# Gathering x1 with its root's inverse and weighting expert rows inside the blocks, in a mixture-of-experts decoder step

## The chip, the cores and the metric

One core of a Trainium2 chip runs the whole step as one program. The metric is device time in microseconds, the median of the runs of one kernel; lower is better.

## What is computed

The kernel is one decoder layer on 576 tokens (512 prompt tokens and 8 x 8 sample tokens) of width 1024, all in fp32:

```
h = rmsnorm(x) * g_mix;  proj = h @ w_in                      # 1024 -> 2560
z_a = b_a * conv3(c_a * v_a);  z_b = silu(layernorm(conv31(v_b * sigmoid(g_b)) + bias))
x1 = x + concat(z_a, z_b) @ w_out
t = rmsnorm(x1) * g_ffn
group = argmax(t @ w_coarse);  two best of that group's 8 experts by t @ w_fine
p = softmax(two best) * softmax(coarse)[group]
x2 = x1 + sum over the two experts e of p_e * ((silu(t @ w_gate[e]) * (t @ w_up[e])) @ w_down[e])
y = rmsnorm(x2) * g_final
```

There are 32 experts of inner width 256: gate, up and down are 1 MB each, 96 MB in all. Four conv histories are outputs as well.

## The kernel before, in words

The semaphores and the order of each engine's instructions are written out by hand; there is no scheduler. The program has these stages.

1. Projection, convolutions and LayerNorm, to about 186 us.
2. Output projection (TensorE), x1 = x + product (DVE), and for each of the five row tiles t of x1: squares and root (ACT), transposes and router logits (TensorE), the choice of experts (DVE), to about 254 us. ACT writes x1 to memory (`x1_rows`, L688), scales it into the normed row h2 with its columns permuted (L712), and writes that too (`h2_rows`, L716).
3. Routing: token-expert rows are sorted into blocks of 64 slots, 30 blocks in this run (of at most 49, `NBLK`). `gidx` says which half row of h2 each of the 128 partitions of a block gathers (64 tokens x 2 halves), `sidx` to which half row of `y_rows` it is scattered. Each token has two y rows, k = 0 and k = 1. The fillers of `keep_busy` (L1457) occupy TensorE between its tasks.
4. The blocks. POOL gathers half rows into `stage[b]` (L887, an indirect DMA; b is the block's number modulo 2). DVE moves a stage to `xrow` (`move`, L1383), TensorE transposes it (`tokens`, L1698), DVE scales it by g_ffn into `xT` (L1387). TensorE multiplies by gate and up (L1707 for a block of one expert, L1712 for one with two), ACT takes SiLU (L748), DVE multiplies (L1394), TensorE transposes (L1722), DVE copies (L1396), TensorE multiplies by down (L1732), ACT copies the result to `yblk[b]` (L752) and POOL scatters it (L917). The expert weights come through eight slots (`places`); SP loads a slot again once its last block is through (`reload`), 24 of 32 experts in this way. The slot in `z` (number 4) shares its rows with `xT`, so its gate and up are loaded in pieces of 1 KB.
5. The end: SP loads x1 back (`xf`, L571), the final gain (L572), the y rows k = 0 once all but the last pair's blocks are scattered (unless a token has both experts in the last pair) and k = 1 once all are (L581). DVE adds for tiles 0 and 4 (`add_row`, L1424); TensorE adds for tiles 1, 2 and 3 by products with the identity (L1786) and with diagonals of the weights (L1794). ACT squares (L775), DVE norms in the order 0, 1, 4, 2, 3 (`normed`, L1437), SP stores (L587).

What sets the order around the change: on SP, loads stand in one queue in program order. On POOL, in a round of the blocks the gather for block g + 4 stands ahead of the scatter of block g. On DVE a round is `block_of`, `tokens_out`, `move`. Lines of the code to which the steps refer:

```
def load_part(i, part, e):                    # L467 (down), L469 (gate, up)
def move(q, b):                               # L1379 to L1383
dve.wait_ge(s_gath[b], q * 16 + 16)
nc.vector.tensor_copy(xrow, stage[b]).then_inc(s_mv, 1)
pool.wait_ge(s_mv, h * 2 + (b + 3))           # POOL's round
gather(h * 2 + (b + 4), b)
scatter(h * 2 + b, b, h * 2 + (b + 2))
```

## Time and profile before

| | |
|---|---|
| median of 3 runs | 518.27 us (517.01 to 520.26) |
| the profiled execution | time 519.05 us, span 517.3 us |
| TensorE busy | 473.6 us, 92% of the span |
| VectorE (DVE) busy | 265.0 us, 51% |
| ScalarE (ACT) busy | 99.9 us, 19% |
| GpSimd (POOL) busy | 193.4 us, 37% |
| read and written | 137.19 MB and 15.53 MB |
| mean granted TensorE clock | 0.985 |

Busy time is that of single engines and overlaps. The span is the part of the execution that the profile covers; the time has a small launch part beside it. A window row gives for each engine its busy time and, in brackets, its instructions. The share of DMA is the mean busy share of the core's 16 DMA engines, and can come out a little over 1.

### The profile page before, as it was taken

To read this page: it belongs to the slowest core of one execution; us is meant where nothing else is said; L and a number is where in the kernel's file an instruction comes from. 1 tells how busy PE (TensorE), PEld (TensorE's weight loads), DVE (VectorE), ACT (ScalarE), POOL (GpSimd) and SP (SyncE) were. 2 spreads that over 40 slices of the span, in tenths; PEclk is the share of its full clock that TensorE was granted. 3 is DMA by queue.
4 is the path that set the end of the run, shared out by engine and by line. 5 is a ranking of instruction groups with operands and counts; after the bars stand their busy time and mean duration, and the time that the engine had idled before them with its cause. 6 is when DMAs were issued, how large, how long until landed. Compare 5 with 4: busy or idle time off the path is not lost.

```text
span 517.3 us, 8897 instructions
## 1 busy us (share of the span) xinstructions
PE 473.6 (92%) x3253; PEld 280.8 (54%) x3254; DVE 265.0 (51%) x559; ACT 99.9 (19%) x202; POOL 193.4 (37%) x289
## 2 busy tenths in 40 slices
PE   7999999999999999999689989999979998989874
PEld 4887777777777735544434434444434444435321
DVE  4209999999999955656841222112212221221226
ACT  5140010110112424324601110111101101110204
POOL 3010925685679830003244433443333334433100
PEclk9989999999999999999699999999999999999999
DMA  8796004300000199869969999999999999999996
GB/s 327 232 378 147 1 3 176 149 1 0 1 0 1 50 384 421 303 223 342 422 272 424 415 415 387 394 407 420 415 386 418 421 420 419 399 405 424 339 322 227
DMA packets 43810, 146.01 MB, mean 282 GB/s; under 512 B 10226, under 2 KB 18434, under 8 KB 32507
## 3 DMA queue, kind: packets, MB, share of 16 engines
q1 hardware_dynamic: 37258, 131.42, 66.1%
q0 software_dynamic: 4960, 9.45, 4.9%
q10 hardware_dynamic: 1561, 4.70, 2.4%
q8 instruction: 22, 0.36, 0.3%
q14 instruction: 9, 0.07, 0.0%
HBM read 137.19 MB, written 15.53 MB: 295 GB/s over the span
## 4 chain that ended last, share of the span: by engine, by line
PE 70%; DMA 10%; issue 7%; DVE 5%; POOL 4%; SPq 2%; ACT 2%; DVEq 0%; POOLq 0%; ACTq 0%
PE banks L1501 26%; PE banks L1712 10%; PE banks L1732 9%; PE banks L1707 9%; PE banks L1559 8%; DMA region_w<-in_w_in 3%; DMA region_x<-in_w_up 2%; DMA region_w<-y_rows 2%; PE banks L1722 2%; PE banks L1588 2%; DVE region_m L1394 2%; DVE region_m L1396 1%; ACT region_m L748 1%; PE banks L1664 1%; DVE slot L1437 1%
## 5 line engine op out<-in xcount | busy, mean ns | idle before, releaser
L1501 PE MATMUL banks<-region_m,region_w 128*128 128x256 f32 (+1 forms) x576 | 141.7, 409 | 0.0
L1501 PEld LDWEIGHTS banks<-region_m,region_w 128*128 128x128 f32 x576 | 110.3, 192 | 30.6 <-issue 0.4
L1394 DVE TENSOR_TENSOR region_m<-region_m,banks 128x128 f32<-128x128 f32 x30 | 8.6, 288 | 159.8 <-ACT region_m L748 159.8
L1030 DVE SCALAR_TENSOR_TENSOR z<-region_m,z 128x512 f32<-128x512 f32 x60 | 49.1, 819 | 0.0
L1030 DVE SCALAR_TENSOR_TENSOR region_x<-region_m,region_x 128x512 f32<-128x512 f32 x56 | 45.8, 818 | 0.0
L825 POOL TENSOR_TENSOR region_m<-region_x 128x512 f32<-128x512 f32 x4 | 20.6, 5138 | 62.0 <-ACT region_m L639 31.8
L1732 PE MATMUL banks<-region_w,region_m 128*32 128x512 f32 x272 | 40.3, 598 | 2.8 <-DVE region_m L1396 2.8
L898 POOL COPY gcol<-gidx 128x1 uint32 (+1 forms) x30 | 5.4, 179 | 95.2 <-DVE region_m L1383 95.2
L627 ACT ACTIVATE region_x<-banks 128x256 f32<-128x256 f32 (+1 forms) x40 | 14.2, 406 | 120.7 <-PE banks L1501 103.6
L887 POOL DMA_INDIRECT region_x<-h_rows,gcol x30 | 31.6, 1052 | 15.2 <-issue 15.2
L752 ACT ACTIVATE region_m<-banks 128x512 f32<-128x512 f32 x30 | 17.9, 597 | 93.6 <-PE banks L1732 93.6
L1707 PE MATMUL banks<-region_w,z 128*64 128x256 f32 x288 | 34.6, 391 | 0.0
L917 POOL DMA_INDIRECT y_rows<-region_m,scol x28 | 28.9, 1032 | 15.1 <-issue 15.1
L1712 PE MATMUL banks<-region_w,z 128*32 128x256 f32 x384 | 30.7, 389 | 0.0
L398 POOL TENSOR_SCALAR region_m<-region_m 128x128 f16<-128x128 f32 x7 | 6.8, 976 | 62.9 <-DVE region_m L1173 49.6
L1559 PE MATMUL banks<-region_w,z 128*128 128x512 f32 x64 | 28.7, 597 | 0.9 <-POOL z L866 0.9
L1707 PEld LDWEIGHTS banks<-region_w,z 128*64 128x64 f32 x288 | 19.6, 134 | 18.3 <-issue 7.5
L748 ACT ACTIVATE region_m<-banks 128x128 f32<-128x128 f32 x30 | 8.3, 277 | 109.7 <-PE banks L1712 66.1
L1732 PE MATMUL banks<-region_m 128*32 128x512 f32 x176 | 25.0, 598 | 1.5 <-DVE region_m L1396 1.5
L1698 PE MATMUL banks<-ident,region_m 128*128 128x128 f32 x124 | 25.2, 286 | 0.5 <-DVE region_m L1383 0.5
L1387 DVE TENSOR_TENSOR z<-banks,gexp 128x512 f32<-128x512 f32 x31 | 21.4, 692 | 0.8 <-PE banks L1698 0.8
L843 POOL TENSOR_TENSOR region_m<-region_x 128x512 f32<-128x512 f32 x4 | 11.7, 2916 | 22.7 <-ACT region_x L627 22.7
(267 smaller groups left out, 704.3 us busy)
## 6 DMA issues: line engine op xcount, KB each, us to landing
region_w<-in_w_down SPq DMA_DIRECT2D x16, 1024.0 KB
region_w<-in_w_gate SPq DMA_DIRECT2D x12, 1024.0 KB, 9.7
region_w<-in_w_up SPq DMA_DIRECT2D x12, 1024.0 KB
region_m<-in_w_down SPq DMA_DIRECT2D x12, 1024.0 KB
region_w<-in_w_in SPq DMA_DIRECT2D x4, 2048.0 KB, 15.8
region_m<-in_w_gate SPq DMA_DIRECT2D x8, 1024.0 KB
region_m<-in_w_up SPq DMA_DIRECT2D x8, 1024.0 KB
region_w<-in_w_out SPq DMA_DIRECT2D x1, 4096.0 KB, 12.9
```

The lines of the kernel that those rows point to most:

```text
L825: pool.tensor_tensor(ub[:, c, HB:HB + SEQ], sv[:, 0:SEQ], sg[:, 0:SEQ], ALU.mult)
L887: pool.indirect_dma_start(stage[b], None, h2_half, bass.IndirectOffsetOnAxis(ap=rows, axis=0), bounds_check=2 * NTOK - 1, oob_is_err=False ...
L917: pool.indirect_dma_start(y_half, bass.IndirectOffsetOnAxis(ap=rows, axis=0), yblk[b], None, bounds_check=4 * NTOK - 1, oob_is_err=False). ...
L1030: last[j % 2] = conv(nc.vector.scalar_tensor_tensor(out=acc[j % 2], in0=ub[:, c, j:j + SEQ], scalar=wB(c, j), in1=acc[j % 2], op0=ALU.mult ...
L1387: nc.vector.tensor_tensor(xT.rearrange("p (h k) n -> p k h n", h=2), ps[0][:, :].rearrange("p (k h n) -> p k h n", k=KC // 2, h=2), gexp[: ...
L1394: nc.vector.tensor_tensor(hid, sg_m, ps[1][:, P:2 * P], ALU.mult).then_inc(s_hid, 1)
L1501: ins = mm(ps[2 * bank + j][:, 0:LEN[j]], sec[name][:, k, c * P:(c + 1) * P], hT[:, k, CUT[j]], start=(k == 0), stop=(k == KC - 1))
L1559: ins = mm(ps[bank][:, :], rows[:, k, :], cols[:, k, :], start=(start and k == 0), stop=(stop and k == KH - 1))
L1698: ins = tr(ps[0][:, k * P:(k + 1) * P], xrow[:, k * P:(k + 1) * P], ident[:, :])
L1707: ins = mm(ps[1][h * T:(h + 1) * T, 0:2 * P].rearrange("p (w f) -> p w f", w=2), xT[:, k, :], wgu[halves[0]][:, :, k, h, :], start=(k == 0 ...
L1712: ins = mm(ps[1][r0:r0 + H, 0:2 * P].rearrange("p (w f) -> p w f", w=2), xT[:, k, half * H:(half + 1) * H], wgu[i][:, :, k, h, :], start=( ...
L1732: ins = mm(ps[3][quarter * H:(quarter + 1) * H, :], hidT[:, c * T + r0:c * T + r0 + H], wdn[halves[quarter % 2]][:, c, h * 512:(h + 1) * 512],
```

## The change

h2 and its rows in memory go. x1 gets rows of 516 words per half: 512 of x1 and four that hold the inverse of its root (the row's normalizing factor). A block gathers such half rows. DVE's `move` takes its columns with a stride of four and multiplies by the factor; ACT copies x1 out of the stage into a PSUM bank (`hold`) so that the stage comes free. ACT's copy of the down product scales each row by its token's weight (`w_row`, found before the blocks by ten matmuls of the lists), DVE adds the held x1 (`add_x1`), and POOL scatters after that. So y rows are x1 + 2 p y, and the end adds two of them: 2 x2, whose final norm has four times the epsilon. The reload of x1, the diagonals and the identity products of x1 are gone.

Since a half of x1 now has features 0 to 511 or 512 to 1023, where a half of h2 had a permuted set, the rows of gate and up are assigned to partitions in two halves, `(h p k)` for `(p k)`: a partition of a load is two pieces of 4 KB where it was one of 8 KB. The slot in `z` still has pieces of 1 KB, now in two DMAs per part.

```diff
-            parts = (a["w_gate"][0].rearrange("e (p k) f -> p e (k f)", k=KC),
-                     a["w_up"][0].rearrange("e (p k) f -> p e (k f)", k=KC),
+            parts = (a["w_gate"][0].rearrange("e (h p k) f -> p e h (k f)", h=2, k=KC // 2),
+                     a["w_up"][0].rearrange("e (h p k) f -> p e h (k f)", h=2, k=KC // 2),
...
-            for t in FINISH:
-                sp.dma_start(xf[0:TROWS[t], t, :], x1_dram[t * P:t * P + TROWS[t], :]).then_inc(s_xf[t], 16)
...
-                nc.scalar.activation(h2[0:n, t % 2, :].rearrange("r (k p) -> r k p", k=KC),
-                                     x1[0:n, t, :].rearrange("r (p k) -> r k p", k=KC), ACT.Copy,
-                                     scale=small[0:n, 32 + t:33 + t]).then_inc(s_h2, 1)
-                act.wait_ge(s_h2, t + 1)
-                act.dma_start(h2_dram[t * P:t * P + n, :], h2[0:n, t % 2, :]).then_inc(s_h2d[t % 2], 16)
+                act.dma_start(x1_dram[t * P:t * P + n, :, :], x1[0:n, t, :, :]).then_inc(s_x1d[t], 16)
...
+            def hold(q, b):
+                act.wait_ge(s_gath[b], q * 16 + 16)
+                if not isinstance(q, int) or q:
+                    act.wait_ge(s_ya, q * 2 + b)
+                nc.scalar.activation(held[b], stage[b][:, 0:HD], ACT.Copy).then_inc(s_held, 1)
...
-                nc.scalar.activation(yblk[b], ps[3][:, :], ACT.Copy).then_inc(s_yc, 1)
+                nc.scalar.activation(yblk[b], ps[3][:, :], ACT.Copy,
+                                     scale=w_row[:, q * 2 + b:q * 2 + b + 1] if isinstance(q, int) else w_row[:, bass.ds(q * 2 + b, 1)])                  .then_inc(s_yc, 1)
...
                 for b in range(2):
-
+                    scatter(h * 2 + b, b, h * 2 + (b + 2))
                     pool.wait_ge(s_mv, h * 2 + (b + 3))
+                    pool.wait_ge(s_held, h * 2 + (b + 3))
                     gather(h * 2 + (b + 4), b)
-                    scatter(h * 2 + b, b, h * 2 + (b + 2))
...
-                nc.vector.tensor_copy(xrow, stage[b]).then_inc(s_mv, 1)
+                nc.vector.tensor_scalar(xrow.rearrange("r (k p) -> r k p", k=KC // 2),
+                                        stage[b][:, 0:HD].rearrange("r (p k) -> r k p", k=KC // 2),
+                                        stage[b][:, HD:HD + 1], None, ALU.mult).then_inc(s_mv, 1)
+
+            def add_x1(q, b):
+                dve.wait_ge(s_held, q * 2 + (b + 1))
+                dve.wait_ge(s_yc, q * 2 + (b + 2))
+                nc.vector.tensor_tensor(yblk[b], yblk[b], held[b], ALU.add).then_inc(s_ya, 1)
...
-            keep_busy(14)
+            pe.wait_ge(s_ohw, 1)
+            pe.wait_ge(s_wq, 1)
+            for i in range(2 * NT):
+                n = TROWS[i // 2]
+                ins = mm(ps[3][:, 0:NBLK], ohw[0:n, i, :], wq[0:n, i, :], start=(i == 0), stop=(i == 2 * NT - 1))
+            ins.then_inc(s_wsum, 1)
+            keep_busy(8)
...
-                nc.vector.scalar_tensor_tensor(out=xf[0:n, t, :], in0=yg[k][t][0:n, :],
-                                               scalar=w12[0:n, k * NT + t:k * NT + t + 1],
-                                               in1=xf[0:n, t, :], op0=ALU.mult, op1=ALU.add)\
-                    .then_inc(s_fin if k else s_fin1, 1)
+                nc.vector.tensor_tensor(xf[0:n, t, :], yg[0][t][0:n, :], yg[1][t][0:n, :], ALU.add).then_inc(s_fin, 1)
```

SP also waits for `w_row` before it loads the last slot (number 7), whose place the lists of the weights occupy.

What stands on DVE in one of the two turns of the loop over blocks, before (L1394 and L1396 are the hidden product and the copy of its transpose, L1387 the tokens' scaling, L1383 the move; names are places in memory, `banks` is PSUM):

```order
L1394 TENSOR_TENSOR region_m<-region_m,banks 128x128
L1396 COPY region_m<-banks 128x128
L1386 REGISTER_ALU
L1387 TENSOR_TENSOR z<-banks,gexp 128x4x2x64
L1380 ISA
L1382 REGISTER_ALU
L1383 COPY region_m<-region_x 128x512
```

The same turn on DVE after the change (L1426, L1428, L1419 and L1408 in the same parts, L1415 is `add_x1`):

```order
L1426 TENSOR_TENSOR region_m<-region_m,banks 128x128
L1428 COPY region_m<-banks 128x128
L1418 REGISTER_ALU
L1419 TENSOR_TENSOR z<-banks,gexp 128x4x2x64
L1415 TENSOR_TENSOR region_m<-region_m,banks 128x512
L1405 ISA
L1407 REGISTER_ALU
L1408 TENSOR_SCALAR region_m<-region_x 128x512
```

The move now stands behind an addition that needs the block's down product and ACT's copy of it.

On POOL, one turn of the loop over blocks before (L898 to L887 are the gather, L906 to L917 the scatter):

```order
L898 COPY gcol<-gidx 128x1
L900 TENSOR_TENSOR carry<-carry 128x1
L887 DMA region_x<-h_rows,gcol 128x512
L905 REGISTER_ALU
L906 ISA
L906 COPY scol<-sidx 128x1
L908 TENSOR_TENSOR carry<-carry 128x1
L917 DMA y_rows<-region_m,scol 2304x512
```

And after it (L928 to L939 are the scatter, L920 to L909 the gather):

```order
L928 COPY scol<-sidx 128x1
L930 TENSOR_TENSOR carry<-carry 128x1
L939 DMA y_rows<-region_m,scol 2304x512
L956 REGISTER_ALU
L920 ISA
L920 COPY gcol<-gidx 128x1
L922 TENSOR_TENSOR carry<-carry 128x1
L909 DMA region_x<-x_rows,gcol 128x516
```

The scatter now stands ahead of the gather.

## Rows read from the trace of the kernel before

**Rows 1.** Windows, the stretch of the blocks: engines' busy time, clock, DMA share, GB/s.
```profile
263.00:487.00 224.00, 201.67 (x2138) 97.08 (x2136) 48.47 (x129) 25.63 (x59) 83.82 (x179) 1.00 1.01 405
```

**Rows 2.** The page, packets of all DMAs.
```profile
DMA packets 43810, 146.01 MB, mean 282 GB/s; under 512 B 10226, under 2 KB 18434, under 8 KB 32507
```

**Rows 3.** Windows of 4 us: PE, PEld, DVE, ACT, POOL, clock, DMA share, GB/s.
```profile
262.00:266.00 4.00, 2.64 (x23) 1.30 (x25) 1.45 (x3) 0.00 (x0) 2.73 (x8) 1.00 0.50 148
...
278.00:282.00 4.00, 4.00 (x36) 1.74 (x33) 0.76 (x2) 0.60 (x1) 1.83 (x6) 1.00 1.02 424
...
310.00:314.00 4.00, 3.78 (x33) 2.08 (x29) 0.29 (x1) 0.47 (x2) 2.11 (x4) 1.00 1.04 354
314.00:318.00 4.00, 3.83 (x47) 1.76 (x51) 1.24 (x3) 0.60 (x1) 1.61 (x4) 1.00 1.09 381
...
334.00:338.00 4.00, 3.46 (x28) 1.06 (x24) 1.53 (x4) 0.36 (x2) 0.41 (x3) 1.00 0.85 311
...
478.00:482.00 4.00, 3.87 (x56) 1.74 (x60) 1.02 (x3) 0.60 (x1) 0.58 (x2) 1.00 1.01 417
482.00:486.00 4.00, 3.48 (x47) 1.58 (x42) 1.52 (x5) 0.28 (x1) 0.61 (x1) 1.00 1.04 317
```

**Rows 4.** Windows, same columns, while only w_out is loaded.
```profile
88.00:92.00 4.00, 4.00 (x18) 3.16 (x17) 3.90 (x6) 0.71 (x2) 3.94 (x4) 1.00 1.02 407
```

**Rows 5.** The chain that ended last: start, us, what.
```profile
453.11 12.41 DMA region_x<-in_w_up
...
488.49 4.86 DMA y_rows<-region_m,slast
...
494.29 11.49 DMA region_w<-y_rows
```

**Rows 6.** Timeline of one block: start, us, engine, line, operation, idle before.
```profile
472.87 3.84 PE L1707 MATMUL banks<-region_x,z 128*64 128x256 f32 x32
473.01 0.60 ACT L752 ACTIVATE region_m<-banks 128x512 f32<-128x512 f32 x1 [3.08 <-PE banks L1732]
473.05 1.05 POOL L887 DMA_INDIRECT region_x<-h_rows,gcol  x1 [0.50 <-issue]
475.11 1.03 POOL L917 DMA_INDIRECT y_rows<-region_m,scol  x1 [0.54 <-issue]
...
476.75 0.44 PE L1698 MATMUL banks<-ident,region_m 128*128 128x128 f32 x2
```

**Rows 7.** Groups by line and shape: count, busy us, mean ns, idle before.
```profile
L1387 DVE TENSOR_TENSOR z<-banks,gexp 128x512 f32<-128x512 f32 x31 | 21.4, 692 | 0.8 <-PE banks L1698 0.8
L1383 DVE COPY region_m<-region_x 128x512 f32<-128x512 f32 x32 | 13.4, 418 | 3.3 <-DMA region_x<-h_rows,gcol 1.9 <-DMA region_x<-h_rows,gidx 1.5
...
L712 ACT ACTIVATE region_m<-region_m,small 128x1024 f32<-128x1024 f32 x4 | 8.6, 2158 | 0.0
L695 ACT ACTIVATE region_m<-region_m 128x1024 f32<-128x1024 f32 x4 | 4.2, 1057 | 34.1 <-DVE region_m L1101 34.1
```

**Rows 8.** Timeline: the third gather and the move that waited for it.
```profile
264.95 1.05 POOL L887 DMA_INDIRECT region_x<-h_rows,gcol  x1 [0.52 <-issue]
...
273.18 0.43 DVE L1383 COPY region_m<-region_x 128x512 f32<-128x512 f32 x1 [1.87 <-DMA region_x<-h_rows,gcol]
```

**Rows 9.** Timeline of the end.
```profile
481.61 1.01 POOL L917 DMA_INDIRECT y_rows<-region_m,slast  x1 [0.54 <-issue]
...
489.50 6.44 SPq L581 DMA_DIRECT2D region_w<-y_rows  x10
...
505.81 1.27 DVE L1424 SCALAR_TENSOR_TENSOR slot<-region_w,w,slot 64x1024 f32<-64x1024 f32 x1 [2.16 <-DMA region_w<-y_rows]
...
512.75 1.28 DVE L1437 SCALAR_TENSOR_TENSOR slot<-banks,small,slot 128x1024 f32<-128x1024 f32 x1
```

**Rows 10.** Timeline of TensorE ahead of the first block.
```profile
260.21 3.19 PE L1457 MATMUL banks<-ident,onesb 128*128 128x512 bf16 x14
...
263.89 0.66 PE L1698 MATMUL banks<-ident,region_m 128*128 128x128 f32 x4 [0.48 <-DVE region_m L1383]
```

More of the change, by code:

```diff
@@ L38 @@
 QR = NS * HB // 2
+HD, XS = D // 2, D // 2 + 4
 NP = KB + KA + 3
@@ L534, in _ @@
             load_part(6, 1, 6)
-            for i in range(2):
-                sp.wait_ge(s_h2d[i], 16 * ((NT + 1 - i) // 2))
             sp.wait_ge(s_x1d[NT - 1], 16)
@@ L1402, in _ @@
             move(0, 1)
-            with nc.vector.Fori(0, pairs) as q:
+            for b in range(2):
+                block_of(0, b)
+                tokens_out(b + 2)
+                add_x1(0, b)
+                move(1, b)
+            with nc.vector.Fori(1, pairs) as q:
                 for b in range(2):
```

189 lines of the change are left out of this document (101 added, 88 removed).

## The prediction

> **What bounds the kernel now.** I read the windows first, then the DMA rates on a fine grid, then the chain of waits and the timeline of one block, and last the end of the span.
>
> From 263 to 487 us, where the 30 blocks run, the DMA engines are busy for the whole time (share 1.01, 405 GB/s) while TensorE is busy for 201.7 of 224 us [rows 1]. Both are near full, but it is the transfers that lead: in the chain, a block waits from 453.11 for an expert's up matrix that lands 12.41 us after its issue [rows 5]. The fine grid shows what the stream does: 424 and 417 GB/s where gate, up and down matrices come in plain form [rows 3]. Each is 1 MB, 8 KB per partition, and 11,303 of the 43,810 packets have 8 KB or more [rows 2]; the code has 96 x 128 - 8 x 128 = 11,264 such rows, so one row is one packet. The two windows in which the slot in `z` is loaded, whose rows are pieces of 1 KB, have 354 and 381 [rows 3]. Once (334 to 338) the stream runs dry for want of a free slot: share 0.85, 311 GB/s, that is (420 - 311) x 4 / 420 = 1.0 us lost.
>
> Behind the blocks DMA is the limit again: between 482 and 486 the weights end, the x1 rows begin, and the rate falls to 317 GB/s at a share of 1.04 [rows 3]. The chain has 4.86 us for the last scatter and 11.49 us for y rows [rows 5].
>
> **The sum.** The profiled execution has a span of 517.3 us and a time of 519.05 us; the median of the runs shown is 518.27 us. I work on the span and move the median by the same amount.
>
> *Gate and up in two pieces of 4 KB (adds).* This isn't named in the change's title, but every gate and up load now has 4 KB rows instead of 8 KB (the slot in `z` keeps 1 KB). w_out is the transfer that looks like the new ones: 4 KB rows, from places 512 KB apart. It ran at 407 GB/s at a share of 1.02 [rows 4]. A line through 1 KB and 8 KB packets gives nearly the same: the two windows of `z` lack (424 - 354 + 424 - 381) x 4 us = 0.45 MB, so 2.1 MB of 1 KB pieces took 6.0 us, 47 ns per packet and engine, against 309 ns for 8 KB at 424; 4 KB then has 159 ns, 411 GB/s. I take 407. Up to the wait at 465.6 the stream carries 40 such loads (slot 7's two, and two for each of the 7 slots outside `z` in three rounds, less the four of the last two slots): 41.9 MB, 99.6 us at 420 and 103.0 us at 407, so +3.4 us. Bounds: 0 (4 KB as good as 8 KB), and 41.9 MB at the 317 GB/s of the x1 rows, also 4 KB pieces [rows 3], +32.6 us. The first value is nearer in form (an input read with many rows per partition) and gets the weight.
>
> The Trainium skill's page "DMA: Bandwidth & Descriptors", section "Why small descriptors are slow (HBM only)", gives a packet a fixed cost of about 3 cycles beside one cycle per 32 bytes. By it 4 KB pieces would be an estimated 1.2% slower than 8 KB, +1.2 us; the trace's 407 against 420 is 3.2%, so the row decides.
>
> *The dry place (takes back).* By 334 us twelve of those loads have passed, 12.6 MB, 1.0 us slower. The stream is then as late as TensorE was early, so the 1.0 us lost there is not lost again, but for the 0.6 us of the next term.
>
> *The start of the blocks.* DVE has a 490-column product (0.7 us, as its products of 512 columns [rows 7]), TensorE ten fp32 matmuls of 49 columns (0.12 us each is my estimate from the transposes of 128 columns, four in 0.66 us [rows 10]), DVE one more small product, and only then the first move. 14 fillers took 3.19 us from 260.21 [rows 10]; now TensorE waits to about 261.4, does 1.2 us of matmuls and 8 fillers of 0.23 us: 264.5 instead of 263.89 for the first transposes, +0.6 us. The gathers start about 0.8 us earlier, since the last rows need no scaled copy of 2.16 us on ACT [rows 7], but the move doesn't, as it stands behind `w_row`. Stream shift in all: +3.4 - 1.0 + 0.6 = +3.0 us. If the clock fell in the new gap, the first block (7 us) would be longer by up to its own length; bound +0 to +7.
>
> *A block's inner work (hidden, with a margin).* After the change DVE adds x1 before it moves the next rows. On the block at 472.87 [rows 6]: down ends, ACT's copy ends at 473.61, the add (PSUM and SBUF, 0.69 as the like one [rows 7]) at 474.4, the move at 475.1: 0.42 us plain [rows 7], 0.6 to 0.7 I take for a strided read; its bounds are 0.42, and twice that, since ACT's strided copy takes 2158 ns against 1057 for a plain pass [rows 7]. TensorE asks for it at 476.75 [rows 6]: 1.6 us to spare, so nothing is added; all 30 blocks would pay whatever goes beyond. ACT holds x1 in PSUM by 475.1, before its next SiLU at 476.8. POOL's gather stood ahead of the scatter; now it stands behind it and starts near 477.5 instead of 473.05 [rows 6]. It must be there before the move 14.2 us after 474.4, at 488.5. A gather under load took 8.2 us, from 264.95 to 273.18 [rows 8]: 485.7, with 2.8 us to spare. Where this cover is gone, what is queued behind is ACT's hold and its SiLU, and DVE's move, and so TensorE.
>
> *Memory traffic.* h2's writes and one set of x1's go (2.36 MB), but all before the stream of the blocks starts, and there DMA stands half idle anyway (share 0.50 from 262 to 266 [rows 3]): 0. Gathered rows have 2,064 bytes, +0.8% of 4.7 MB: 0.04 MB, 0.1 us. The same page, section "How a descriptor splits into AXI transactions", has reads begin on 256-byte boundaries, which these rows mostly miss; by it the gathers would cost an estimated 12% more beats, up to 1.4 us. No row here shows it.
>
> *The end (gain).* Let T be the end of the last down product: 487.0 before, 490.0 after. Before: the scatter issued at 481.61 was landed at 489.5, when SP asked for the first y rows [rows 9]; x1's 2.36 MB were in the way of it and of everything behind. The second y row tile of t = 4 was added at 505.81 = T + 18.8, and then DVE's five norms ran without a gap, last start 512.75, end T + 27.0 [rows 9]; with the output's landing T + 30.3. After: no x1 rows. The last weights are in at about T - 3.6, the final gain at T - 2.1; the scatter before the last is issued at 481.61 - T + 0.75 = T - 4.7 (the add stands in its way) and lands near T - 1 in quiet queues. First y rows: 2.36 MB at 317 GB/s, 7.5 us, from T + 1.3 to T + 8.8. The last scatter is issued 0.75 us later than before, T + 2.2, and lands 4.86 us later [rows 5], T + 7.1. Second y rows behind it, from T + 9.2: t = 0, 1 and 4 are 1.31 MB, 4.1 us, T + 13.3. One add of 1.28 us, five norms of 1.39 us: T + 21.6, and 3.3 us for the output: T + 24.9. Against T + 30.3 that is -5.4 us. The diagonals (DVE) and the identity products (TensorE) were waiting for transfers anyway: 0 by themselves. Bounds: -2 us if the second y rows take as long as before behind the last scatter, -7 us if they run at 400 GB/s.
>
> Sum: +3.0 - 5.4 = -2.4 us. 518.27 - 2.4 = **515.9 us**.
>
> **Rivals.**
> 1. *Pieces cost nothing.* If the stream is limited by bytes, T is 487.6 (only the start's 0.6, less what the dry place took), and the end gives 5.4 to 7: 518.3 + 0.6 - 6.4 = 512.5 us. For it: share 1.02 for both sizes. Against: 1 KB pieces plainly lower the rate [rows 3].
> 2. *The strong stream cost (the other side).* Gate and up in 4 KB pieces run below 395 GB/s. 41.9 MB cost 106.1 us there, +6.5, and the net is about nothing (+0.7); at 370 GB/s, +13.6, so 518.3 + 13.6 - 0.4 - 5.4 = 526.1 us. For it: 317 GB/s on x1 rows of 4 KB [rows 3]. Against: 407 of w_out [rows 4].
> 3. *The end stays.* x1's rows were hidden in the wait for the last scatter, and only 2 us go: 518.3 + 3.0 - 2 = 519.3 us. For it: the first y rows were asked for only when the scatter had landed. Against: the share there is 1.02 to 1.04, so bytes count.
> 4. *Late gathers.* A gather that needs over 11 us stalls ACT, DVE and TensorE; each microsecond over is paid up to 30 times. 1 us: 516 + 15 to 30, about 538 us. Against: 2.8 us of margin.
>
> **How the numbers follow.** Forecast (net -1 to -4 us): 0.45. Rival 1: 0.22. Rival 2: 0.14. Rival 3: 0.14. Rival 4: 0.05. Half a rival at each end is outside: the range is 510.5 to 524. A measurement of this kernel tells about 1% from no change, 5.2 us. Faster by over that is most of rival 1 and a little of the forecast: 0.27. Slower by over that: rival 4 and half of rival 2 and more, 0.15. Within it: 0.58.
>
> **What would show it.** In the profile after: 4 us windows of the stream at 405 to 410 GB/s (424: rival 1; under 395: rival 2); no dry window near 334; TensorE's last down near 490; DVE's move 0.6 to 0.7 us, with no idle time behind a gather; the last norm's end some 21 to 22 us behind T. More than 5% of idle time of TensorE in front of its transposes of tokens, or of ACT's SiLU behind a gather, would prove me wrong in the blocks; a T under 488 in the stream; and an end longer than 27 us in the last term.

## The result

| | before | after |
|---|---|---|
| median, same chip | 518.34 us (517.01 to 520.26, 4 runs) | 526.02 us (525.50 to 526.29, 4 runs) |
| profiled execution: span, mean granted clock | 517.3 us, 0.985 | 523.6 us, 0.973 |

The change makes the kernel slower: ratio 1.0144, 95% interval 1.0111 to 1.0177, +7.7 us. Forecast was 515.9 us, in a range up to 524. A second comparison on another chip (a_again, below) gave 1.0114 (1.0069 to 1.0158).

Three stretches of one execution say where the time went. *Start* is from DVE's write of `gidx` to its first copy of a transposed hidden block (L1396 before, L1428 after), *blocks* from there to the last such copy, *end* from there to the start of the last norm.

| us | start | blocks | end | together |
|---|---|---|---|---|
| before | 11.4 | 214.4 | 28.0 | 253.7 |
| after | 17.4 | 218.6 | 23.8 | 259.8 |
| difference | +6.0 | +4.2 | -4.2 | +6.1 |

What lies ahead of `gidx` (259.0 and 259.2 us) and behind the last norm (4.6 us in both) is alike, so this is nearly the whole of the span's +6.3. (The differences are taken before rounding.)

The kernel after, windows (engines' busy time, then TensorE's granted clock, DMA share and GB/s), for [rows 1] and [rows 3]:

```profile
262.00:266.00 4.00, 4.00 (x23) 2.96 (x22) 1.16 (x6) 0.98 (x2) 1.65 (x6) 0.69 0.48 140
266.00:270.00 4.00, 3.12 (x13) 1.52 (x15) 0.99 (x2) 0.14 (x1) 1.25 (x2) 0.50 0.90 307
270.00:274.00 4.00, 4.00 (x44) 2.02 (x43) 0.29 (x1) 0.00 (x0) 1.41 (x3) 0.53 1.00 399
...
278.00:282.00 4.00, 4.00 (x37) 2.02 (x30) 1.29 (x2) 1.29 (x2) 0.78 (x3) 1.00 1.02 406
...
294.00:298.00 4.00, 3.56 (x54) 1.84 (x46) 1.71 (x4) 0.90 (x3) 2.09 (x5) 1.00 0.13 46
298.00:302.00 4.00, 3.84 (x35) 1.67 (x36) 1.69 (x4) 0.88 (x2) 1.11 (x2) 1.00 1.00 323
...
334.00:338.00 4.00, 3.98 (x36) 1.82 (x38) 1.61 (x3) 0.99 (x2) 1.18 (x2) 1.00 1.00 405
...
278.00:462.00 184.00, 166.41 (x1726) 79.64 (x1718) 61.26 (x124) 39.20 (x75) 77.45 (x149) 1.00 1.01 394
```

Two things are new. From 262 to 274 TensorE's granted clock is between 0.50 and 0.69: it ran at its lower level, 1.2 GHz, for most of that time, where before it had 1.00 [rows 3]. And at 294 to 298 the stream is dry: share 0.13 and 46 GB/s; that window and the next lack (410 - 46 + 410 - 323) x 4 / 410 = 4.4 us of the stream. Elsewhere it runs about as forecast: the two windows shown have 405 and 406 GB/s (405 to 410 expected; single windows from 282 to 294 have 407 to 420), and the dry place of before at 334 [rows 3] is gone.

The packets, for [rows 2]; the many of 4 KB are now counted under 8 KB:

```profile
DMA packets 50498, 141.35 MB, mean 270 GB/s; under 512 B 10322, under 2 KB 18530, under 8 KB 46363
```

The timeline ahead of the first block after the change, for [rows 10] (start, us, engine, line, operation, idle time before):

```profile
259.70 0.17 PE L1800 MATMUL banks<-region_m,onesb 64*32 64x1 bf16 x1
...
260.80 0.67 DVE L1382 TENSOR_TENSOR region_m<-region_m 128x490 f32<-128x490 f16 x1
...
261.62 2.98 PE L1805 MATMUL banks<-region_m 128*128 128x49 f32 x20 [1.74 <-DVE region_m L1382]
...
264.53 3.60 PE L1487 MATMUL banks<-ident,onesb 128*128 128x512 bf16 x8
264.63 0.21 DVE L1432 TENSOR_TENSOR w_row<-banks,region_m 128x49 f32<-128x49 f32 x1 [2.20 <-PE banks L1805]
264.76 0.68 DVE L1408 TENSOR_SCALAR region_m<-region_x 128x512 f32<-128x512 f32 x1
...
267.91 1.06 PE L1729 MATMUL banks<-ident,region_m 128*128 128x128 f32 x4
```

TensorE stands idle for 1.74 us for the weighted lists (L1382), then does the ten matmuls (20 records) in 2.98 us, where I had 1.2. The 8 fillers behind them take 0.45 us each (3.60 / 8), twice the 0.23 us of [rows 10], and the transposes 1.06 us against 0.66: that is half clock. The first transposes of tokens start 4.0 us later than before, and the first block, at half clock, loses two more: its gate and up products take 5.66 us where they took 3.83.

Not all of the 6.0 us is the clock. In the profile of a_fill (below) the clock is 1.00 in this stretch; there the ten matmuls take 2.53 us, the 8 fillers behind them 1.90 us, and the transposes come 1.8 us later behind `gidx` than before. By that row some 1.8 us of the start are the added work itself, and some 4.2 us the low clock.

Groups of the blocks after the change (count, busy us, mean ns, idle before), for [rows 7]:

```profile
L1408 DVE TENSOR_SCALAR region_m<-region_x 128x512 f32<-128x512 f32 x32 | 21.8, 682 | 0.0
L1419 DVE TENSOR_TENSOR z<-banks,gexp 128x512 f32<-128x512 f32 x31 | 21.4, 692 | 3.6 <-PE banks L1729 3.6
L1415 DVE TENSOR_TENSOR region_m<-region_m,banks 128x512 f32<-128x512 f32 x30 | 20.6, 688 | 70.2 <-ACT region_m L766 70.2
L766 ACT ACTIVATE region_m<-banks,w_row 128x512 f32<-128x512 f32 x30 | 20.6, 688 | 96.1 <-PE banks L1763 96.1
L757 ACT ACTIVATE banks<-region_x 128x512 f32<-128x512 f32 x32 | 19.2, 602 | 30.1 <-DVE region_m L1415 24.8 <-DVE w_row L1432 5.3
```

The strided move takes 682 ns, the add 688, the held copy 602. The move has no idle time before it (0.0), so no gather was late: rival 4 did not come. Blocks follow each other at 7.0 to 7.2 us in this kernel (7.0 to 7.1 before), wherever no block waits for weights.

The blocks' +4.2 us lie at those that wait. By the time from hidden copy to hidden copy, the 6th block gives back 1.1 us (7.4 for 8.5), the 28th adds 2.9 (11.9 for 8.9), and the others together 2.4, none over 0.8. The 28th has two parts. Its first product before, in the timeline:

```profile
465.62 0.39 PE L1712 MATMUL banks<-z 128*32 128x256 f32 x1 [1.60 <-DMA region_x<-in_w_up]
```

The same product after, and the windows around it:

```profile
474.33 0.39 PE L1743 MATMUL banks<-z 128*32 128x256 f32 x1 [3.09 <-DMA region_x<-in_w_up]
```

```profile
472.00:476.00 4.00, 1.67 (x24) 1.14 (x28) 1.28 (x2) 0.77 (x2) 2.07 (x5) 0.89 1.02 408
476.00:480.00 4.00, 4.00 (x49) 2.24 (x39) 0.00 (x0) 0.18 (x1) 1.06 (x1) 0.68 1.03 411
```

TensorE waits 3.09 us for the up matrix, 1.5 us longer than before, and then the clock falls a second time (0.89 and 0.68; before it stayed at 1.00 here), so that the block's gate and up products take 5.4 us for 4.0.

The chain of waits (start, us, what), for [rows 5], and the end's timeline, for [rows 9]:

```profile
461.53 12.71 DMA region_x<-in_w_up
...
499.88 4.56 DMA y_rows<-region_m,slast
...
505.38 6.61 DMA region_w<-y_rows
```

```profile
492.75 1.02 POOL L939 DMA_INDIRECT y_rows<-region_m,slast  x1 [0.15 <-issue]
...
495.15 12.74 SPq L594 DMA_DIRECT2D region_w<-y_rows  x10
...
499.88 1.01 POOL L939 DMA_INDIRECT y_rows<-region_m,slast  x1 [0.16 <-issue]
...
512.08 1.22 DVE L1458 TENSOR_TENSOR slot<-region_w 64x1024 f32<-64x1024 f32 x1 [2.23 <-DMA region_w<-y_rows]
...
518.96 1.28 DVE L1468 SCALAR_TENSOR_TENSOR slot<-banks,small,slot 128x1024 f32<-128x1024 f32 x1
```

The wait for y rows fell from 11.49 us [rows 5] to 6.61. The last down product ends at T = 497.4 (487.0 before; 490.0 was forecast), the add of t = 4 starts at T + 14.7 (y rows were to be in at T + 13.3) and the last norm ends at T + 22.8 (forecast 21.6; 27.0 before [rows 9]).

### The profile page after: what moved, and what is told of

The parts are those of the page before. It is cut to its first block, busy times and chain, and to the rows that moved or that the text cites. A ratio compares the mean times of both kernels' runs of the same rounds, so it can differ in the third digit from the quotient of the medians.

```text
span 523.6 us, 9093 instructions
## 1 busy us (share of the span) xinstructions
PE 473.9 (91%) x3255; PEld 282.0 (54%) x3256; DVE 290.8 (56%) x586; ACT 112.8 (22%) x230; POOL 202.2 (39%) x290
## 4 chain that ended last, share of the span: by engine, by line
PE 62%; DMA 9%; issue 8%; SPq 7%; DVE 7%; POOL 4%; ACT 2%; DVEq 0%; POOLq 0%; ACTq 0%
PE banks L1531 26%; PE banks L1763 8%; PE banks L1589 8%; PE banks L1743 7%; PE banks L1738 4%; SPq L486 3%; DMA region_w<-in_w_in 3%; DMA region_x<-in_w_up 2%; SPq L481 2%; PE banks L1695 1%; PE banks L1753 1%; PE banks L1619 1%; DVE region_m L1428 1%; DMA region_w<-y_rows 1%; DVE slot L1468 1%
## 5 line engine op out<-in xcount | busy, mean ns | idle before, releaser
L1415 DVE TENSOR_TENSOR region_m<-region_m,banks 128x512 f32<-128x512 f32 x30 | 20.6, 688 | 70.2 <-ACT region_m L766 70.2
L928 POOL COPY scol<-sidx 128x1 uint32 x28 | 13.3, 476 | 94.5 <-DVE region_m L1415 94.5
L1426 DVE TENSOR_TENSOR region_m<-region_m,banks 128x128 f32<-128x128 f32 x30 | 8.6, 288 | 71.9 <-ACT region_m L762 48.1
L847 POOL TENSOR_TENSOR region_m<-region_x 128x512 f32<-128x512 f32 x4 | 20.0, 5004 | 62.4 <-ACT region_m L652 31.7
L766 ACT ACTIVATE region_m<-banks,w_row 128x512 f32<-128x512 f32 x30 | 20.6, 688 | 96.1 <-PE banks L1763 96.1
L909 POOL DMA_INDIRECT region_x<-x_rows,gcol x30 | 31.7, 1057 | 15.3 <-issue 15.3
L939 POOL DMA_INDIRECT y_rows<-region_m,scol x28 | 29.0, 1035 | 15.1 <-issue 15.1
L1743 PE MATMUL banks<-region_w,z 128*32 128x256 f32 x384 | 32.5, 401 | 0.3 <-issue 0.3
L1589 PE MATMUL banks<-region_w,z 128*128 128x512 f32 x64 | 28.8, 597 | 0.8 <-POOL z L888 0.8
L757 ACT ACTIVATE banks<-region_x 128x512 f32<-128x512 f32 x32 | 19.2, 602 | 30.1 <-DVE region_m L1415 24.8
L1419 DVE TENSOR_TENSOR z<-banks,gexp 128x512 f32<-128x512 f32 x31 | 21.4, 692 | 3.6 <-PE banks L1729 3.6
## 6 DMA issues: line engine op xcount, KB each, us to landing
region_w<-in_w_gate SPq DMA_DIRECT2D x12, 1024.0 KB, 11.9
```

The source lines that it names most:

```text
L766: nc.scalar.activation(yblk[b], ps[3][:, :], ACT.Copy, scale=w_row[:, q * 2 + b:q * 2 + b + 1] if isinstance(q, int) else w_row[:, bass.ds ...
L909: pool.indirect_dma_start(stage[b], None, x1_half, bass.IndirectOffsetOnAxis(ap=rows, axis=0), bounds_check=2 * NTOK - 1, oob_is_err=False ...
L939: pool.indirect_dma_start(y_half, bass.IndirectOffsetOnAxis(ap=rows, axis=0), yblk[b], None, bounds_check=4 * NTOK - 1, oob_is_err=False). ...
L1415: nc.vector.tensor_tensor(yblk[b], yblk[b], held[b], ALU.add).then_inc(s_ya, 1)
L1419: nc.vector.tensor_tensor(xT.rearrange("p (h k) n -> p k h n", h=2), ps[0][:, :].rearrange("p (k h n) -> p k h n", k=KC // 2, h=2), gexp[: ...
L1589: ins = mm(ps[bank][:, :], rows[:, k, :], cols[:, k, :], start=(start and k == 0), stop=(stop and k == KH - 1))
```

## Experiments

The theory after the traces: (1) the clock fell in the wait and the thin matmuls ahead of the first block, the block came 6 us late, slots came free late, and the stream ran dry; (2) the 4 KB pieces cost 2 to 3 us; (3) the end gives back some 4. The rivals: it is the lateness of `w_row`'s chain itself, whatever the clock; it is the pieces alone; or the work in the blocks is not hidden. Single profiled executions of one kernel differ by some 3 us, partly in what lies ahead of `gidx` (written at 258.0 to 263.4 us in these profiles), so the ratios (each with its interval against the kernel before on the same chip) decide, and the stretches say where.

| kernel | median us | ratio (95%) | start | blocks | end |
|---|---|---|---|---|---|
| a_again | 524.85 | 1.0114 (1.0069 to 1.0158) | 14.7 | 216.3 | 24.8 |
| a_fill | 522.18 | 1.0048 (1.0017 to 1.0079) | 14.5 | 218.1 | 24.1 |
| a_best | 522.46 | 1.0059 (1.0035 to 1.0083) | 13.9 | 216.9 | 24.4 |
| a_hold | 520.59 | 1.0021 (0.9996 to 1.0046) | 13.5 | 216.4 | 24.8 |
| a_nochain | 521.63 | 1.0060 (1.0033 to 1.0087) | 11.5 | 220.5 | 24.1 |
| a_8k | 526.19 | 1.0111 (1.0049 to 1.0172) | 17.4 | 214.7 | 27.3 |
| a_fill_8k | 519.29 | 1.0000 (0.9977 to 1.0023) | 13.0 | 214.4 | 25.8 |
| a_hold_8k | 519.18 | 0.9996 (0.9972 to 1.0019) | 13.6 | 214.1 | 24.6 |
| a_xf | 529.25 | 1.0175 (1.0127 to 1.0222) | 16.1 | 217.1 | 28.8 |
| a_hold_xf | 525.74 | 1.0123 (1.0093 to 1.0152) | 13.8 | 216.5 | 29.7 |
| b_4k | 521.79 | 1.0049 (1.0025 to 1.0072) | 11.6 | 216.7 | 28.7 |
| b_nofill | 521.46 | 1.0033 (1.0006 to 1.0059) | 13.9 | 214.7 | 27.1 |
| b_late | 520.55 | 1.0015 (0.9994 to 1.0036) | 13.2 | 213.1 | 28.5 |
| b_noxf | 517.65 | 0.9974 (0.9948 to 1.0000) | 11.4 | 215.8 | 24.3 |
| b_noxf2 | 517.03 | 0.9953 (0.9935 to 0.9972) | 11.4 | 216.4 | 23.7 |

Kernels that begin with a_ are the changed one with an edit, those with b_ the one before with an edit.

### The cold start

**a_fill**: TensorE has work while it waits.

```diff
+            keep_busy(8)
             pe.wait_ge(s_ohw, 1)
             pe.wait_ge(s_wq, 1)
```

> The changed kernel with 8 more fillers on TensorE before it waits for the weighted lists (the gap of 1.7 us at 259.9). Cold-start theory (the clock fell to half there and made the first block 6.2 us late, which let the stream of weights run dry for 3.5 us at 294): the clock stays at full, the first hidden copy is at about 271 instead of 276.6, no dry window, time about 521.5 us (4.5 less than the changed kernel). Pieces theory (4 KB pieces of gate and up are what costs): the clock changes too, but the stream is the limit, time stays within 1.5 us of 526.0.

1.0048 against 1.0144 and 1.0114 of the unchanged one: eight fillers, 2 us of added work, made the kernel 3.4 to 5 us faster (0.66% to 0.96% of 518, each figure uncertain by 2 to 3 us). The profile does not show the rest of what I expected. The profiled execution was the slowest of its ten, 526.67 us. Its clock is 1.00 from 262 to 278 us, through the ten matmuls, but in the first block TensorE then stands idle for 1.88 us, the clock is 0.59 from 278 to 282, the first hidden copy comes 14.5 us behind `gidx`, and the stream has 38 GB/s from 298 to 302.

**b_nofill**: the same in the other direction, on the kernel before.

```diff
-            keep_busy(14)
             pe.wait_ge(s_tab, 1)
```

> The kernel before without the 14 fillers ahead of the first block (260.2 to 263.4), so that TensorE stands still there. Cold-start theory: granted clock at half in the first block, its hidden copy some 2 to 3 us late, the stream dry at 290 to 298, time +1.5 to +3 us (520.5). Pieces theory: no change, since the transfers are the limit, 518.3.

Windows of b_nofill:

```profile
262.00:266.00 4.00, 1.12 (x4) 0.72 (x4) 1.27 (x6) 0.00 (x0) 2.52 (x9) 0.75 0.41 76
266.00:270.00 4.00, 3.54 (x36) 1.89 (x40) 0.80 (x2) 0.00 (x0) 1.99 (x4) 0.50 1.01 423
270.00:274.00 4.00, 3.42 (x46) 1.80 (x42) 0.79 (x3) 0.28 (x1) 0.00 (x0) 0.89 1.01 419
```

Without the fillers TensorE is busy for 1.12 of 4 us, and the clock of the next window is 0.50. The first transposes come 4.9 us behind `gidx` as before, so the start's 13.9 us for 11.4 are the clock's; the time rises by 1.7 us (0.33%, interval 0.3 to 3.1), as the theory had it. So the clock alone can do this, without any new chain.

**a_nochain**: no lists of weights, no matmuls, 14 fillers as before; the down products are scaled by the reciprocal of the token's number in place of its weight.

```diff
-            nc.scalar.activation(ohw, ohr, ACT.Copy).then_inc(s_ohw, 1)
...
-            nc.vector.tensor_tensor(wq, ohq, w_tile.rearrange("p t k -> p (t k)").unsqueeze(2).to_broadcast([P, 2 * NT, NBLK]),
-                                    ALU.mult).then_inc(s_wq, 1)
+            nc.vector.tensor_copy(w_row, vnum).then_inc(s_wrow, 1)
...
-            for i in range(2 * NT):
...
-                ins = mm(ps[3][:, 0:NBLK], ohw[0:n, i, :], wq[0:n, i, :], start=(i == 0), stop=(i == 2 * NT - 1))
...
-            keep_busy(8)
+            keep_busy(14)
```

> The changed kernel without the chain of w_row (no weighted lists, no ten matmuls; 14 fillers as before; every row is weighted by its token number, so y is not the reference's). Cold-start theory: as a_best, ratio 0.997 within 0.004, clock at full in the first block. Rival (blocks): 1.005 or above.

The start is 11.5 us again (11.4 before), and the window from 294 to 298 has 407 GB/s: no dry place there. The ratio is 1.0060, so the chain with all that follows from it costs 2.8 to 4.4 us (1.0114 and 1.0144 less 1.0060). But 1.0060 is not the 0.997 that I expected: it is the ratio of the rival. The blocks took 220.5 us in its profile, the longest of all, and 4.5 us of the 6.1 over before are at block 28 (13.4 us from copy to copy, 8.9 before): TensorE waited 3.49 us there for the up matrix, 1.9 longer than before, and then did the gate and up products in 6.6 us for 4.0, at a clock of 0.50. So even with a full clock at the start the changed kernel isn't back at the time of before, and here the clock fell later.

**a_best**: 8 fillers ahead of the matmuls and none behind; the move of block 0 and the held copies stand ahead of `w_row`, which only ACT's first scaled copy needs.

```diff
+            keep_busy(8)
             pe.wait_ge(s_ohw, 1)
...
             ins.then_inc(s_wsum, 1)
-            keep_busy(8)
...
-            dve.wait_ge(s_wsum, 1)
-            nc.vector.tensor_tensor(w_row, ps[3][:, 0:NBLK], vnum, ALU.mult).then_inc(s_wrow, 1)
             move(0, 0)
+            dve.wait_ge(s_wsum, 1)
+            nc.vector.tensor_tensor(w_row, ps[3][:, 0:NBLK], vnum, ALU.mult).then_inc(s_wrow, 1)
...
-            act.wait_ge(s_wrow, 1)
             for b in range(2):
                 hold(0, b)
+            act.wait_ge(s_wrow, 1)
```

> The changed kernel with the start of the blocks reordered: 8 fillers on TensorE in the gap before the weighted lists, none behind the ten matmuls; DVE moves the first rows before it makes w_row; ACT holds the first two stages before it waits for w_row. Cold-start theory (clock and the chain of w_row ahead of the first block are the larger part of the loss): from gidx to the first hidden copy 11.5 us as in the kernel before (17.4 in the changed one), no dry window at 294, and with the pieces' cost and the shorter end left over a time 1 to 2 us under before, about 517 (ratio 0.997). Rival, that the loss is in the blocks (late gathers, DVE's longer turn): ratio stays at 1.005 or above.

1.0059: no better than a_fill, and on the rival's side of 1.005; the 0.997 that I expected did not come. The clock was 1.00 from 262 to 266 us, through the ten matmuls, and 0.57 from 266 to 270: behind the matmuls TensorE now stood idle for 0.56 us for the move, with no fillers there.

**a_hold**: as a_best, with one filler behind every second of the ten matmuls and four behind the last.

```diff
                 ins = mm(ps[3][:, 0:NBLK], ohw[0:n, i, :], wq[0:n, i, :], start=(i == 0), stop=(i == 2 * NT - 1))
+                if i % 2 == 0:
+                    keep_busy(1)
             ins.then_inc(s_wsum, 1)
-            keep_busy(8)
+            keep_busy(4)
```

> The changed kernel with 8 fillers ahead of TensorE's wait, one filler behind every second of the ten matmuls, 4 behind them, and the first move and holds ahead of w_row. Theory (the clock fell because TensorE had little to do while it waited and during the ten matmuls): the clock stays at 1.00 from 262 us, the first hidden copy comes 12.0 to 13.0 us behind gidx (11.4 before, 17.4 in the changed kernel), ratio 1.000 to 1.005. Rival (the time was lost by w_row's chain being late, whatever the clock): ratio 1.006 to 1.012.

Windows of a_hold:

```profile
262.00:266.00 4.00, 4.00 (x29) 3.18 (x28) 1.28 (x6) 1.20 (x2) 2.14 (x8) 1.00 0.46 156
266.00:270.00 4.00, 3.12 (x46) 1.97 (x48) 1.28 (x2) 0.00 (x0) 1.94 (x4) 1.00 0.92 341
...
290.00:294.00 4.00, 3.58 (x58) 1.96 (x50) 1.58 (x4) 1.04 (x3) 2.08 (x5) 1.00 0.85 342
294.00:298.00 4.00, 3.83 (x34) 1.60 (x34) 1.68 (x4) 0.75 (x2) 1.06 (x1) 1.00 0.97 333
```

The clock stays at 1.00, the dry place shrinks to (410 - 342 + 410 - 333) x 4 / 410 = 1.4 us, and the ratio is 1.0021. The same sums, with a few fillers more and the first move and holds ahead of `w_row`, are 4.8 us faster on the same chip than the changed kernel (1.0114), 6.4 by the first comparison, each uncertain by 2 to 3 us. Against a_best, which has the same order without the fillers among and behind the matmuls, it is 2.0 us, uncertain by 1.8. What the new order gives by itself isn't shown. The start is 13.5 us, not the 12 to 13 that I gave; the ratio is as the theory had it, and the rival's 1.006 did not come.

**a_again**: the changed kernel itself, on the chip of a_hold.

> The changed kernel once more, on the same chip as its variants. If the first comparison was sound, the ratio is 1.011 to 1.018. The granted clock should again be under 0.7 for some 8 us after the ten matmuls (262 to 274 us), and the first hidden copy 16 to 18 us behind the write of gidx.

```profile
262.00:266.00 4.00, 3.08 (x22) 2.69 (x23) 1.97 (x11) 0.02 (x1) 2.46 (x6) 0.90 0.41 68
266.00:270.00 4.00, 3.35 (x12) 1.35 (x10) 1.00 (x3) 1.10 (x2) 1.43 (x3) 0.67 0.75 309
...
294.00:298.00 4.00, 3.42 (x42) 1.48 (x38) 1.20 (x3) 0.29 (x2) 2.70 (x6) 1.00 0.61 178
```

The clock falls again, for a shorter time in this execution (0.90, 0.67), the start has 14.7 us and the dry window 178 GB/s where a longer fall gave 46. The start I expected, 16 to 18 us, was that of one execution.

**b_late**: is it the clock or the lateness? 14 more fillers at full clock ahead of the first block of the kernel before.

```diff
             keep_busy(14)
+            keep_busy(14)
```

> The kernel before with 28 fillers in place of 14: TensorE reaches the first transposes some 3.2 us later, at full clock. Theory (a late first block is a late first reload, and the stream of weights sets the end): the first hidden copy comes about 3 us later than before and the time rises by 2 to 3 us, ratio 1.004 to 1.006. Rival (the first blocks have slack, and only a low clock costs): under 0.5 us, ratio under 1.001.

```profile
290.00:294.00 4.00, 3.56 (x54) 1.85 (x46) 0.57 (x3) 0.28 (x1) 1.54 (x4) 1.00 0.97 375
294.00:298.00 4.00, 3.94 (x34) 1.74 (x36) 0.96 (x3) 0.60 (x1) 1.81 (x5) 1.00 0.94 363
...
334.00:338.00 4.00, 3.60 (x32) 1.61 (x32) 1.53 (x4) 0.28 (x1) 0.94 (x2) 1.00 0.98 340
```

Neither of my two numbers: the start is 1.8 us longer, the blocks 1.3 us shorter, the time +0.8 us (interval -0.3 to +1.9). Block 6 waits for its weights before (8.5 us from copy to copy), and 7.3 here: that wait takes in the first 1.2 us of lateness. My reading is that what goes beyond it is paid once, as a dry place (here 375 and 363 GB/s from 290 to 298). By this price, an estimate from one pair of profiles, a start that is 2 us late costs under 1 us, one that is 6 us late some 5. No run has a start 6 us late at full clock. b_nofill's start is 2.5 us late and costs 1.7, and there block 6 took in 1.5 us.

### The pieces of 4 KB

**b_4k**: only the pieces, in the kernel before (with the two DMAs per part for the slot in `z`); h2's columns and g_ffn are permuted to match, so the sums are the same.

```diff
-            parts = (a["w_gate"][0].rearrange("e (p k) f -> p e (k f)", k=KC),
+            parts = (a["w_gate"][0].rearrange("e (h p k) f -> p e h (k f)", h=2, k=KC // 2),
...
-                                     x1[0:n, t, :].rearrange("r (p k) -> r k p", k=KC), ACT.Copy,
+                                     x1[0:n, t, :].rearrange("r (h p k) -> r h k p", h=2, k=KC // 2), ACT.Copy,
```

> The kernel before with gate and up in two pieces of 4 KB (h2's columns permuted to match) and nothing else of the change. Pieces theory as forecast: windows of the stream at 405 to 410 GB/s, T at 489.5, time 520.7 us (+2.4). If pieces are the cause of the whole loss: +8 or more, 526. If only the cold start matters: within 1 us of before.

+2.5 us (interval 1.3 to 3.7), as forecast (+2.4). Its profiled execution has a span 4.2 us longer than before, 2.4 of it in the blocks, and 2.2 of those at block 28, where TensorE waited 3.77 us for the up matrix (1.60 before) with the clock at 1.00. The same stretch of the stream in the kernel before, in b_4k and in a_hold, each from its own windows:

```profile
278.00:462.00 184.00, 167.10 (x1766) 80.08 (x1761) 38.05 (x101) 21.85 (x50) 70.98 (x150) 1.00 1.02 409
```

```profile
278.00:462.00 184.00, 167.08 (x1766) 81.01 (x1766) 38.13 (x100) 21.71 (x50) 70.97 (x150) 1.00 1.03 405
```

```profile
278.00:462.00 184.00, 165.16 (x1734) 79.13 (x1734) 60.89 (x124) 38.56 (x74) 77.58 (x148) 1.00 1.03 401
```

409 and 405 GB/s: 1.8 us over these 184 (a mean in which downs, gathers and scatters keep their form). The changed kernel had 394 there, 6.7 us less of the stream than before, and with the clock held 401, 3.6 us less.

**a_8k**, **a_fill_8k**, **a_hold_8k**: the changed kernel, a_fill and a_hold with gate and up in 8 KB rows. The rows of the weights then meet the wrong features of x1; the work is otherwise the same.

```diff
-            parts = (a["w_gate"][0].rearrange("e (h p k) f -> p e h (k f)", h=2, k=KC // 2),
+            parts = (a["w_gate"][0].rearrange("e (p k) f -> p e (k f)", k=KC),
```

> The changed kernel with gate and up loaded in 8 KB pieces as before (the rows of the weights are then assigned to the wrong features, every transfer and operation is the same in size). Pieces theory: windows of the stream back at 420 GB/s, 3.5 us or more of the 7.7 go, about 522. Cold-start theory: the stream only runs dry earlier and longer near 294, less than 2 us go, about 524.5.

> The changed kernel with the 8 fillers in the gap and 8 KB pieces of gate and up (weights' rows assigned to the wrong features). If cold start and pieces add up, as their effects from gidx to the last hidden copy in the single looks (3.4 and 3.9 us) say: ratio 1.0052 less 2.4 to 3.9 us, 0.998 to 1.0005. If one hides the other: 1.003 or above.

> a_hold with gate and up in 8 KB rows again (the rows then go to the wrong features). If the +0.2% that a_hold keeps is the pieces (2.5 us) against what the end gives back, this one is 2 to 3 us faster than a_hold: ratio 0.996 to 0.998, and it would be the first version with the new blocks that is not slower than before. Rival (the work added to the blocks costs something that no row names): 0.999 to 1.003.

The blocks take 214.7, 214.4 and 214.1 us, as before (214.4), whatever else was changed. The sum alone would prove little, as waits differ: block 28 waits less than before (7.2 to 7.6 us from copy to copy for 8.9) and block 16 more (10.9 to 11.9 for 9.3). But where no block waits the copies are 7.0 to 7.2 us apart, for 7.0 to 7.1 before, so at most 0.1 us of the blocks' new work comes through in each. In time the 8 KB rows are worth 0.2 to 1.7 us with the cold start (a_8k against the two measurements of the changed kernel), 2.5 us in a_fill and 1.3 us in a_hold; each of the last two is uncertain by some 2 us, the first by over 3. a_8k stays 1.1% slower than before, slower than both of my numbers for it: the pieces alone are not the cause. a_fill_8k has the ratio that I expected if cold start and pieces add up. a_hold_8k, 0.9996, has the ratio of the rival that I wrote for it (the blocks' work costs), though its blocks' 214.1 us speak against that; its interval holds both.

### The end

**b_noxf**, **b_noxf2**: the kernel before without x1's reload (the sum lacks x1), in 3 and in 5 rounds.

```diff
-            for t in FINISH:
-                sp.dma_start(xf[0:TROWS[t], t, :], x1_dram[t * P:t * P + TROWS[t], :]).then_inc(s_xf[t], 16)
```

> The kernel before without the reload of x1 at the end (5 transfers, 2.36 MB; the sum lacks x1). Forecast's term for the end: the end from T becomes 5.4 us shorter, the time 513 (ratio 0.990); what the changed kernel shows from T to the last norm is 4.4 us. Rival 3 (the reload was hidden in the wait for the last scatter): 2 us or less, 516.5.

> b_noxf once more, in five rounds: the kernel before without x1's reload, the sum lacking x1. Theory (the reload costs 3.5 to 4 us, and the first measurement of 1.35 was low by the scatter of the stream): ratio 0.992 to 0.995. Rival (mostly hidden): 0.996 to 0.999.

The chain of b_noxf2:

```profile
493.72 4.50 DMA y_rows<-region_m,slast
...
499.16 7.10 DMA region_w<-y_rows
```

-1.35 us in time (interval -2.7 to 0) and -2.4 (-3.4 to -1.5): by the first the rival holds, the second lies between theory and rival. The end is 3.7 and 4.3 us shorter in the profiles (the y rows 7.10 us, for 11.49 in [rows 5]), but in both the blocks are longer, by 1.4 and 2.1 us, since block 28 comes 11.0 us behind the one ahead of it, for 8.9 before. TensorE waited hardly longer there (2.06 and 2.12 us for 1.60), but its clock fell behind the wait, and the gate and up products took 5.6 us for 4.0:

```profile
464.00:468.00 4.00, 2.56 (x34) 1.75 (x38) 0.00 (x0) 0.13 (x1) 1.97 (x4) 0.84 1.03 428
468.00:472.00 4.00, 3.67 (x39) 2.02 (x32) 0.29 (x1) 0.28 (x1) 0.00 (x0) 0.74 1.01 411
```

So the reload was not hidden at the end, and part of its gain went in a fall of the clock 20 us ahead of the edit. There is one profile of the kernel before; how often its own clock falls there isn't known.

**a_xf**, **a_hold_xf**: the reload put back into the changed kernel and into a_hold; nothing uses what is read, but the adds and norms wait for it.

```diff
+            for t in FINISH:
+                sp.dma_start(xf[0:TROWS[t], t, :].rearrange("r (h d) -> r h d", h=2), x1_dram[t * P:t * P + TROWS[t], :, 0:HD]).then_inc(s_x1d[t], 16)
```

> The changed kernel with x1's reload put back (its rows are read into the tile and then overwritten; the adds and norms wait for them). It prices in the changed kernel what the end saved by not reading x1. By my forecast's end term, 5.4 us less what is not the reload: 4 to 5 us more than the changed kernel. Rival (the reload was mostly hidden, as leaving it out of the kernel before gave only 1.35 us): 1 to 2 us more than the changed kernel.

> a_hold with x1's reload put back as in a_xf: prices the reload without the cold start in the way. Theory (4 us, as last hidden copy to last norm went from 27.9 to 24.8 us): ratio 1.008 to 1.011. Rival (mostly hidden, 1.35 us by b_noxf): 1.004 to 1.006.

a_xf is 4.4 us slower than a_again by the medians, but 3.2 by the ratios (0.6%), uncertain by 3.4: not clear of noise. a_hold_xf is 1.0% slower than a_hold, 5.3 us, uncertain by 2, more than the 4 us of the theory. The end is 4.0 and 4.9 us longer in the profiles. The windows of a_hold_xf and its timeline show part of the reason:

```profile
494.00:498.00 4.00, 0.00 (x0) 0.00 (x0) 0.00 (x0) 0.34 (x2) 0.03 (x1) 0.50 0.86 323
498.00:502.00 4.00, 1.06 (x2) 0.58 (x3) 0.00 (x0) 0.00 (x0) 0.00 (x0) 0.50 1.01 336
502.00:506.00 4.00, 4.00 (x6) 1.61 (x5) 0.00 (x0) 0.00 (x0) 0.00 (x0) 0.50 1.05 354
```

```profile
500.94 8.21 PE L1838 MATMUL banks<-region_w,ident 128*128 128x512 f32 x12 [10.37 <-DMA region_w<-y_rows]
```

TensorE was idle for 10.37 us, and the first of its twelve identity products of y ran at half clock, on the chain that ended last; the next twelve took 5.31 us. The products of x1 which the change removed had kept it busy there in the kernel before (clock 1.00 and 3.02 us busy from 486 to 490, 3.28 from 490 to 494). So this experiment prices the reload together with a cold stretch. Only part of that is new: in a_hold itself TensorE is idle for 3.64 us at this place, the clock is 0.63 from 494 to 498, and the same twelve products take 7.08 us. The reload adds 1.1 us to them, so the 5.3 us are rather too high a price.

## Why the prediction was wrong

It was wrong: 7.7 us slower, outside the range, where 2.4 us faster was forecast. By its own steps:

1. **"The start of the blocks" (+0.6) is the step that failed.** Measured: start +6.0 us in the first profile and +3.3 in the second (a_again); against a_hold, whose clock holds there, the changed kernel loses 4.8 to 6.4 us of time. Of the 6.0 us some 4.2 are the granted clock, which was 0.69, 0.50 and 0.53 where I counted with 1.00. I saw the mechanism ("If the clock fell in the new gap, the first block (7 us) would be longer by up to its own length; bound +0 to +7."), took the lower end without a row for it, and gave it no rival. [Rows 10] could have warned: the kernel before has 14 fillers in that very place. The other 1.8 us are there at full clock too, three times my 0.6: the ten matmuls take 2.53 us at full clock and took 2.98 (I had 0.12 us each, from transposes). The fillers were counted at 0.23 us, which holds at full clock only.
2. **"The dry place (takes back)" fell with it.** I held that a later stream only eats TensorE's lead. That is right for a stream that is slow by itself (b_4k has no dry window at 290 to 298, 410 and 413 GB/s). But when TensorE is late the slots come free late, and the stream stops: 46 GB/s, 4.4 us. The place at 334 was filled, as forecast; a new one stood 40 us ahead of it. The slack is what block 6's wait takes in: 1.2 us in b_late, 1.5 in b_nofill and a_hold. b_late shows a lower rate for 1.8 us of lateness at full clock (375 and 363 GB/s from 290 to 298, for 400 and 422 before); that the 6 us of the changed kernel made its window of 46 is my reading of it.
3. **Pieces of 4 KB (+3.4, less 1.0): right.** b_4k measured +2.5 us; the stream has 405 GB/s from 278 to 462 us, and single windows of 4 us up to 298 have 409 to 420. (41.9 MB at 407 against 420 GB/s are 3.2 us; the 3.4 was a slip.) Rival 1 (pieces cost nothing) and rival 2 (under 395 GB/s, the one on the slow side) both fell: the result landed at rival 2's 526.1 us for another reason. The Trainium skill's page "DMA: Bandwidth & Descriptors", section "Why small descriptors are slow (HBM only)", would have 4 KB an estimated 1.2% slower than 8 KB, 1.2 us; b_4k's whole interval (1.3 to 3.7 us) lies above that, by little at its lower end. In the forecast's traffic term, 12% more beats for the gathers is the most that the Trainium skill's page "DMA: Bandwidth & Descriptors", section "How a descriptor splits into AXI transactions", gives: a row of 2,064 bytes that starts up to 240 bytes behind a boundary takes 65 to 72 beats for the 64 of before, an estimated 7% in the mean. No run shows it.
4. **Block's inner work (0): right.** Move 682 ns (0.6 to 0.7 forecast), add 688, no idle time behind a gather, and copies 7.0 to 7.2 us apart where no block waits.
5. **The end (-5.4): the right sign, too large.** -4.2 us by the stretches. The add and the later scatter cost 1.0 us (last hidden copy to last scatter: 3.7 us before, 4.7 after), 0.25 more than I had, and y rows 0 and 1 landed 1.4 us later behind T than forecast (T + 14.7). Rival 3 (hidden) doesn't hold for the end: the reload is worth 3.7 and 4.3 us of it in b_noxf and b_noxf2. In time only 1.35 and 2.4 us came out there, with 1.6 us lost in both profiles to the clock in block 28.
6. **The clock behind later waits (no term in the forecast).** Where the up matrix of block 28 came 2.1 to 3.8 us after TensorE was free, the clock fell to 0.50 in five of the profiles: after, b_nofill, b_noxf, b_noxf2 and a_nochain. The gate and up products then took 5.4 to 6.6 us for 3.8 to 4.1. Behind waits of 1.5 to 1.9 us it stayed at 1.00, but also behind 2.83 us in a_xf and 3.77 us in b_4k, so the length of the wait alone doesn't decide it, and what does stays open.

In the two profiles the differences are: start +6.0 (clock 4.2, added work 1.8), block 6 -1.1, block 28 +2.9 (wait 1.5, clock 1.5), the other blocks +2.4, the end -4.2; together +6.1 with rounding. The pieces have no line of their own in this account. They are part of the waits, above all of block 28's, where b_4k has nearly all of its +2.4 in the blocks; so their price of 2.5 us can't be added to these lines. What set the long wait at block 28 in this execution isn't shown: it is 3.09 us here, but 1.91 in a_again, the same program, and 1.87 in a_hold. It isn't shown either what remains in a_hold: its 0.21% is within the noise (-0.04% to +0.46%), and a start 2.1 us longer, the pieces and a shorter end have both signs. No version that computes the reference was measurably faster than the kernel before.
